# Low halves of weight slabs on GpSimd, layer-norm sums and ScalarE's order of copies in a two-block model on one Trainium2 core

## What is computed

```python
# first block, T = 272
n1 = rmsnorm(h)
xr, gr, cq, ckv, kr, g_rnn, g_att = split(n1 @ w_in)
y_rnn = (rg_lru(causal_conv4(xr)) * gelu(gr)) @ w_rnn_out
y_att = mla_attention(rmsnorm(cq) @ w_uq, rmsnorm(ckv) @ w_ukv, rope(kr)) @ w_attn_out   # 16 heads
h = h + (sigmoid(g_rnn) * y_rnn + sigmoid(g_att) * y_att) @ w_out
q = rmsnorm(h) @ w_q                          # 8 heads, 2 x 128 keys, top 16 of each half, top 16 of pairs
h = h + sum(softmax(top) * gelu(u[idx] . x) * v[idx])
x = rmsnorm(h)[16:]
# second block, T = 256
x += .5 rms(swiglu(rms(x)));  x += rms(conformer_conv(rms(x)));  x += .5 rms(swiglu(rms(x)))
x += .5 rms(swiglu(rms(x)));  x += rms(moba(rms(x)) @ w_o);      x += .5 rms(swiglu(rms(x)))

def conformer_conv(h):
    a, g = split(h @ w_in + b_in)
    u = depthwise_conv31(a * sigmoid(g)) + b_dw          # causal, per channel
    mu, var = mean(u), mean((u - mu) ** 2)               # over the 1024 channels
    return silu((u - mu) * rsqrt(var + eps) * ln_g + ln_b) @ w_out + b_out
```

## Time and profile before

| | |
|---|---|
| median of 3 runs | 2160.17 us (2159.29 to 2160.92) |
| profiled execution | 2159.29 us, of which the span 2158.0 |
| granted TensorE clock, mean | 0.993 of full |
| busy: TensorE, VectorE, ScalarE, GpSimd | 2109.6, 1599.5, 1196.8, 294.8 us |
| share of the span | 98%, 74%, 55%, 14% |
| read from memory | 352.86 MB, 164 GB/s |
| chain that ended last | TensorE 84%, VectorE 11%, ScalarE 2% |

### The profile page before, as it was taken

The page is one execution under the profiler, slowest core; times in us unless marked ns, Lnnn a source line. Parts: engine busy times, 40 slices in busy tenths (PEclk is TensorE's granted clock), DMA queues, the critical chain, the costliest instruction groups (busy, mean ns, idle before and its releaser), DMA issues.

```text
span 2158.0 us, 41607 instructions
## 1 busy us (share of the span) xinstructions
PE 2109.6 (98%) x17096; PEld 2014.1 (93%) x17096; DVE 1599.5 (74%) x2700; ACT 1196.8 (55%) x2106; POOL 294.8 (14%) x281
## 2 busy tenths in 40 slices
PE   9999999999999999999999999989999999999997
PEld 9899999999999988888889998989999999899997
DVE  7887768899987599965568647968656764788664
ACT  6776666454433444445557755865445545565453
POOL 7101023232000000000013001032001101113001
PEclk9999999999999999999999999999999999999999
DMA  5533555555545544555555564225554655544553
GB/s 174 164 127 98 167 170 176 180 181 182 169 150 167 173 164 162 168 186 194 194 168 185 184 197 136 73 88 174 188 196 138 195 187 195 185 135 150 190 193 116
DMA packets 101132, 357.17 MB, mean 166 GB/s; under 512 B 12048, under 2 KB 15440, under 8 KB 100816
## 3 DMA queue, kind: packets, MB, share of 16 engines
q1 hardware_dynamic: 100080, 352.35, 49.5%
q10 hardware_dynamic: 864, 2.16, 0.3%
HBM read 352.86 MB, written 1.05 MB: 164 GB/s over the span
## 4 chain that ended last, share of the span: by engine, by line
PE 84%; DVE 11%; ACT 2%; DMA 1%; issue 1%; POOL 0%; SPq 0%; ACTq 0%; DVEq 0%; POOLq 0%
PE PS L325 84%; DVE wlo L413 3%; DMA raw<-stream 1%; DVE H L2725 1%; DVE bn L2676 1%; ACT whi L333 1%; DVE H L2723 1%; DVE act L1767 1%; DVE act L1814 1%; DVE XC L1063 0%; DVE act L1818 0%; DVE act L1810 0%; ACT bsq L333 0%; PE PS L721 0%; DVE act L1784 0%
## 5 line engine op out<-in xcount | busy, mean ns | idle before, releaser
L413 DVE TENSOR_TENSOR wlo<-raw,whi 128x1024 fp32r<-128x1024 f32 x643 | 804.4, 1254 | 211.2 <-ACT whi L333 210.6
L333 ACT ACTIVATE whi<-raw 128x1024 fp32r<-128x1024 f32 (+1 forms) x667 | 698.7, 1051 | 189.2 <-PE PS L325 101.3
L325 PE MATMUL PS<-bn,whi 128*128 128x256 f32 x3328 | 595.3, 281 | 16.2 <-ACT bn L333 8.7
L325 PEld LDWEIGHTS PS<-bn,whi 128*128 128x128 f32 x3328 | 510.5, 188 | 21.7 <-issue 12.0
L325 PE MATMUL PS<-n,whi 128*128 128x256 f32 (+1 forms) x2784 | 508.6, 284 | 4.9 <-DVE wlo L410 2.8
L325 PE MATMUL PS<-bn,wlo 128*128 128x256 f32 x1664 | 459.5, 280 | 0.0
L325 PEld LDWEIGHTS PS<-n,whi 128*128 128x128 f32 x2784 | 429.0, 189 | 9.1 <-issue 4.3
L325 PE MATMUL PS<-n,wlo 128*128 128x256 f32 (+1 forms) x1392 | 391.8, 281 | 0.0
L325 PE MATMUL PS<-whi,c 128*128 128x512 f32 x1024 | 324.7, 393 | 0.6 <-ACT act L333 0.6
L325 PEld LDWEIGHTS PS<-bn,wlo 128*128 128x128 f32 x1664 | 313.3, 188 | 0.0
L325 PEld LDWEIGHTS PS<-n,wlo 128*128 128x128 f32 x1392 | 263.2, 189 | 0.0
(11 more groups left out here) (351 smaller groups left out, 2750.3 us busy)
## 6 DMA issues: line engine op xcount, KB each, us to landing
raw<-stream SPq DMA_DIRECT2D x666, 512.0 KB, 3.3
abias<-c_alibi ACTq DMA_DIRECT2D x1, 1536.0 KB, 6.5
H<-xt SPq DMA_DIRECT2D x4, 256.0 KB, 6.7
out<-H SPq DMA_DIRECT2D x3, 256.0 KB, 2.2
mask<-c_mask SPq DMA_DIRECT2D x1, 272.0 KB, 6.5
K<-Vh SPq DMA_DIRECT2D x2, 136.0 KB, 4.3
K<-Vl SPq DMA_DIRECT2D x2, 136.0 KB, 4.4
out<-H ACTq DMA_DIRECT2D x2, 128.0 KB, 1.9
```

The source lines that it names most:

```text
L325: return self.nc.tensor.matmul(out, l, r, start=start, stop=stop, skip_group_check=True)
L333: return self.nc.scalar.activation(out, in_, func, **kw)
L413: k.s[q].inc(me.e.tensor_tensor(lo[:, :], raw[:, :], hi[:, :].bitcast(F32), ALU.subtract))
```

## The change

It has four parts.

1. `lo_by_pool`: GpSimd gets slabs 10, 12, 14, 16, 18, every third from 21 to 345 and 417, 420, 423, 426, 429. The 22 slabs of before are among them; 97 are new, and VectorE has as many fewer.
2. The sums of the layer norm: chunks 4, 5, 0, 1, 6 are added up by GpSimd (`add(i)`, 8 additions into `k.acc` and `z.ysum`), and TensorE sums `acc`, `ysum` and chunks 2 and 3 at tap (3, 27) and chunk 7 behind the last tap: 8 matmuls in place of 16.
3. `act_post`: for banks m from `rows` on, the copies due for bank m's last tile go ahead of bank m's read (before: those due for bank m-2, and the rest behind the last bank). With `rows` 0 nothing changes.
4. `ACC_FREE["postc"]`: GpSimd waits for `ln_sum` there, since `acc` is now read later.

```diff
-CENTRE_A, CENTRE_B, SUMS_A, SUMS_6 = (2, 6), (3, 20), (3, 0), (3, 12)
+CENTRE_A, CENTRE_B, SUMS_AT = (2, 6), (3, 20), (3, 27)
 def lo_by_pool(s):
-    return PLAN.at["u", 0] <= SLAB * s < PLAN.at["u", NKEY // 2] and s % 3 == 0
+    return (10 <= s <= 18 and s % 2 == 0) or (21 <= s <= 345 and s % 3 == 0) or (417 <= s <= 431 and s % 3 == 0)
-            "postc": ("sums", SUMS["prec"]), "pre1": ("stds", STDS["postc"]), "post1": ("sums", SUMS["pre1"]),
+            "postc": ("ln_sum", 3), "pre1": ("stds", STDS["postc"]), "post1": ("sums", SUMS["pre1"]),
+POOLED = [FIRST_PE, FIRST_PE + 1, 0, 1, FIRST_PE + 2]
# TensorE
-    def sums(chunks):
-        for i in chunks:
-            first, last = i == FIRST_PE, i == NC - 1
+    def sums_so_far():
+        P.wait_ge(s["ln_acc"], len(POOLED) - 1)
+        P.wait_ge(s["stds"], STDS["prec"])
+        k.mm(PS[:, 6, 0:NX], k.ones, k.acc, True, False)
+        P.wait_ge(s["ln_ysum"], len(POOLED) - 1)
+        k.mm(PS[:, 7, 0:NX], k.ones, z.ysum, True, False)
+        for i in (2, 3):
             P.wait_ge(s["cen"], CENTRED[i])
...
-            if (i, t) == SUMS_A:
-                P.wait_ge(s["stds"], STDS["prec"])
-                sums((FIRST_PE, FIRST_PE + 1, 0, 1))
-            if (i, t) == SUMS_6:
-                sums((FIRST_PE + 2,))
-    sums((2, 3, NC - 1))
+            if (i, t) == SUMS_AT:
+                sums_so_far()
+    P.wait_ge(s["cen"], CENTRED[NC - 1])
+    s["ln_sum"].inc(k.mm(PS[:, 6, 0:NX], k.ones, c.w[:, NC - 1, :], False, True))
+    P.wait_ge(s["cen_q"], CENTRED[NC - 1])
+    s["ln_sum"].inc(k.mm(PS[:, 7, 0:NX], k.ones, z.sq[:, NC - 1, :], False, True))
# ScalarE, act_post
-            ring.to(at((*key, m if rows == 0 else max(m - 2, rows)), kx - 1))
+            ring.to(at((*key, m), kx - 1))
...
-    ring.to(at((*key, NC - 1), kx - 1))
# GpSimd, pool_conv
+    def add(i):
+        q, first = POOLED[i], i == 1
+        b = POOLED[0]
+        if first:
+            G.wait_ge(s["sums"], SUMS["prec"])
+            G.wait_ge(s["cen"], CENTRED[b])
+        else:
+            G.wait_ge(s["ln_acc"], i - 1)
+        G.wait_ge(s["cen"], CENTRED[q])
+        s["ln_acc"].inc(pool.tensor_tensor(k.acc, c.w[:, b, :] if first else k.acc, c.w[:, q, :], ALU.add))
+        if not first:
+            G.wait_ge(s["ln_ysum"], i - 1)
+        G.wait_ge(s["cen_q"], CENTRED[q])
+        s["ln_ysum"].inc(pool.tensor_tensor(z.ysum, z.sq[:, b, :] if first else z.ysum, z.sq[:, q, :], ALU.add))
+    for i in range(1, len(POOLED)):
+        add(i)
```

## The result

The changed kernel is slower: 2175.18 us median (2169.7 to 2178.76, 6 runs) against 2159.51 (2154.0 to 2160.92, 6 runs), ratio 1.0082, 95% interval 1.0062 to 1.0100. The forecast was 2165.0, the range 2153 to 2172: the direction was right, the size about a third of what came, and the time lies above the range. The profiled execution took 2176.31 us, span 2175.0.

A forecast was written before the change was run, and what follows sets the result against it. The prediction took TensorE as the bound, busy 2109.6 of 2158.0 us. Its terms, 3.5 - 1.1 + 1.0 + 4.0 - 1.9 + 0.2 = +5.7 us on 2159.29, gave 2165.0; range for 8 in 10, 2153 to 2172.

The forecast's parts named there:

- Price of a moved slab: Low halves moved to GpSimd: each costs a full VectorE 0.87 us, mean loss 2.0 against relief of 1.13.
- Step 1: Slabs 10 to 18, first block: new stall on GpSimd's low half of slab 10 and later VectorE, +3.5 us.
- slab 13's: First block: the existing 1.30 us stall at 61.24 on slab 13's low half was to come later, not earlier.
- Step 2: Slabs 21 to 153: relief of VectorE shortens TensorE's gap before `K`, -1.1 us; output projections 0.
- Step 3: Slabs 154 to 345, rest of u and v: VectorE just fills up and falls behind, +1.0 us.
- Step 4: Slabs 417 to 429 and layer-norm sums: later VectorE and a TensorE wait on squares of chunk 2 or 3, +4.0 us.
- My formula: Layer-norm sums: 8 GpSimd additions each lengthen VectorE's taps, 8 x 0.52 = 4.2 us.
- D: VectorE's lateness at the end of its taps and centres, from moved slabs and GpSimd additions: 7.7 us.
- Step 5: ScalarE's copy order in two post-norms: posta -1.9 us, postc +0.2 us.
- (c): Rival: clearly slower, VectorE saturates in u and v, +8 there, 2172 us; chance 0.14.
- (a): Rival: faster, exclusion costs little and gains at `K`, cin, sums and posta stand, 2152.5 us; chance 0.26.
- (b): Rival: no change that can be told, exclusion at 1.5 us a slab, 2158 to 2161 us; chance 0.18.

The follow-up runs named there:

- lo_memset: lo_only's slab list, but GpSimd writes zeros to the low halves instead of subtracting, against the kernel before: 0.9969, -6.7 us.
- lo_only: Only the slab list changed against the kernel before (97 more low halves on GpSimd), sums and ScalarE's order as before: 1.0054, +12 us.
- first_only: Only slabs 10, 12, 14, 16, 18 moved to GpSimd against the kernel before, whose 22 stay: 1.0007 (0.9989 to 1.0024).
- fill_only: Every third slab from 21 to 89 moved to GpSimd beside the 22 of the kernel before, nothing else changed: 1.0010 (0.9998 to 1.0023).
- ln_only: Only the layer-norm sums changed against the kernel before (8 GpSimd additions, 8 matmuls fewer): 1.0016, +3.5 us.
- ln_four: ln_only with chunk 6 taken out of GpSimd's sum (6 additions, TensorE sums chunk 6), against the kernel before: 1.0004 (0.9990 to 1.0018).

## Why the prediction was wrong

- **Price of a moved slab.** The exclusion was the right mechanism (lo_memset shows it, with the reserve on the shorter instruction). But I had it cost by VectorE's load, 0.87 us of lateness a slab on a full engine. In the mean that was too high: VectorE's busy time rose by 15.5 us for 97 slabs in lo_only, 0.16 a slab. And what a slab costs TensorE depends on which step it meets: u's second half at 98% lost nothing, the fill at some three quarters lost 4.
- **Step 1**, +3.5: +3.7 in the changed kernel, about 3 above kernels without those slabs. Right in size, and its stall on GpSimd's low half is there in first_only (1.05); the rest of the loss, behind three stretched L1063, is a case of the price, at another place than slab 13's.
- **Step 2**, -1.1, is the step that failed first and by most: it became +4.0 (fill_only +3.3), 5.1 of the 11.3 us by which the span missed the forecast. "The other rows before `K` read one operand from PSUM" is false: the scan XR<-R,XC stands between and has two SBUF operands. It took 2.69 for 0.70 and turned the relief into a longer wait. Time was lost further on: "0, hidden under TensorE's own stream" for slabs 50 to 89 priced only the low half's own arrival, not the gate and `o` steps that it stretches, and nothing was allowed for a second stretch at half clock.
- **Step 3**, +1.0: v +1.84, u +0.07. The nearness is luck: no overflow of load made TensorE wait. The time went in six stretched one-hot steps, which the step doesn't have.
- **Step 4**, +4.0: cin +3.22 and LN +4.89, 4.1 more. Two terms were missing. My formula had the additions only lengthen taps (which they did: 21 taps took 10.82 for 8.39). I priced what GpSimd does to VectorE and not what VectorE does to GpSimd, though the earlier trace rows showed GpSimd at 3.29 for 2.41. The last addition took 6.25, TensorE waited for it and not for the squares that I had named, and the clock of the sums was halved: ln_only +4.07 where the gain should have been 2.7. And that slab 426 stands behind `uhl` I had written down and given no price; TensorE waited 2.23 for it. D, my 7.7 us of lateness, was too large a term: lo_only's LN is -0.02 with the old sums, and the changed kernel's is 0.82 above ln_only's with the new ones.
- **Step 5**: posta -1.85 for -1.9. Postc +1.33 for +0.2, the bound of one copy exceeded, since the landing of the slab (1.40) and half clock came on top; it is +0.13 and -1.03 elsewhere, so its size hangs on when the slab lands.
- **Rivals.** (c) has the time nearest to the result, by another way: VectorE's load made TensorE wait nowhere in u's second half. (a) is refuted for this change; its gains at `K` and in cin appear only when GpSimd doesn't read, that of posta in every kernel with the new order. (b)'s 2158 to 2161 lies outside the interval.

Open are the rule that gives one of the two engines the turn, what decides the landing of postc's slab, and the first block by time. No kernel with the changed slab list and ln_four's sums was run, nor one with slab 426's low half ahead of `uhl`.

## What to carry to other kernels

Before work is moved to GpSimd, list the VectorE instructions that can run beside it, and look for two-operand ones on a chain that another engine waits for; relief counts only where VectorE's queue is what is waited for, the stretching counts at every such chain. Look also at what stands ahead of the moved work in GpSimd's own program. Do not put a small GpSimd step on the path while VectorE has a run of independent two-operand instructions: it may get no turn until the run ends. And read the granted clock behind a long wait of TensorE: the one of 4.16 us was paid again in the sums at clock 0.50.

## What the runs showed of the hardware that I had not expected

- A 256-column GpSimd addition took 6.25 us beside 13 back-to-back VectorE taps (twice, in two kernels), 0.76 to 0.92 beside taps where it followed its own predecessors at once.
- A scan (0.70 to 2.69), a bf16 comparison with a broadcast operand (0.68 to 2.30) and a gate product (0.41 to 1.72) are all stretched beside GpSimd's subtraction, none beside its memset of 957 ns.
- After TensorE's waits of 3.56 and 4.16 us the sums ran at half clock (1.06 for 0.59), after one of 0.89 they didn't. Behind the wait of 3.47 at 180.63 the clock stayed up for 1.4 us and fell then (0.50 from 182.2 to 185.1).
- 97 low halves of 1.25 us taken from VectorE, and nothing else changed, raised its busy time by 15.5 us (lo_only); with a memset on GpSimd in their place it fell by 130.9 us.
